# The mixers' order on three engines: scores, gelu, pool parts, transposes, out chunks and the taps of a convolution

## The chip, the cores and the metric

The kernel runs on one core of a Trainium2 chip. The metric is the device time of one execution in microseconds (us). TensorE is PE here, VectorE DVE, ScalarE ACT, GpSimd POOL, SyncE SP.

## What is computed

Two blocks of two layers each on a sequence of 256 tokens of width 1024. The first block has gated feed-forward parts around a forgetting attention and a dilated attention. The second block, twice, runs a mixer of four branches and a feed-forward part with a short convolution. The change touches the mixer alone:

```python
def second_block(x, ...):
    for l in range(DEPTH):                       # 2
        z = rms_norm_2(x, norm_mix_pre[l]) @ w_in[l]
        za, zq, zkv, zg, zc, zd = jnp.split(z, offsets, axis=-1)
        y_conv = conformer_conv(za, ...)         # a*sigmoid(gate), causal conv of 31 taps, layer norm, silu
        y_nsa = nsa_attention(q, ...)            # 4 heads: selected, windowed and compressed keys
        y_sgu = spatial_gating(zc, ...)          # gelu, layer norm of one half, 128x128 products in time
        y_pool = multiscale_pool(zd, ...)        # running means of 2, 4, 8, 16 and a product
        y = jnp.concatenate([y_conv, y_nsa, y_sgu, y_pool], axis=-1) @ w_out[l]
        x = x + rms_norm_2(y, norm_mix_post[l])
        ...
```

## The kernel before

All weights come as one stream of quarters of 128x1024, loaded by SP into a ring. Each quarter q is split in two for products of the precision wanted: ACT rounds it (split, L1055, w_hi), DVE subtracts (split, L1461, ring_lo), and PE makes three products of each pair, low by high, high by low, high by high (quarter, L444 to L446). ACT may split quarter q once PE is done with q-4; a split of DVE follows ACT's. There is no scheduler: each engine's program is a hand-written order, with waits on semaphores, and an engine does its instructions in that order. So what stands behind a wait waits too.

In mixer(l) quarters 0 to 15 of it (part(j, r), four 512-wide column groups j) make z; quarters 16 to 23 are the output product, cut in chunks of 128 rows in the order pool (chunks 0 and 1), gating (2 and 3), attention (4 and 5), convolution (6 and 7). out_chunk(kk) is quarter 16+kk; the last three are done in down_last (L499 to L501). The pieces of which this text speaks:

- Attention: compressed() (L891, L892) makes the compressed keys; DVE copies them (L2040, L2041, kv_ready). scores(0) and scores(1) (L920, L925) are the scores of two heads each. For each head h DVE takes masked maxes(h) (L1962), ACT exps(h) (L1307), DVE weigh(h) (L1969, L1971), ACT weighed(h) (L1317, six parts), PE turn_probs(h) (L937, L940), DVE take_probs(h) (L1978, L1979), PE values(h) (L949 to L951). PE's turn_probs(0) writes where part(3, r) was summed, so it waits for the gelu's read of it.
- Pool: pooled() (L863), ACT's copy pT (L1346), mixed() (L871), ACT's pool_hi (L1357), DVE's pool_out (L2066). out_chunk(0) waits for pool_out.
- Gating: the gelu of part 3 (L1353, b_gelu), DVE statistics (L2058, L2061), ACT's root (L1361), DVE's norm (L2073 to L2081), gating() (L898), DVE's product ysg (L2091), turn_gating (L906), ACT's sgu_hi (L1369), DVE's sgu_out (L2098). out_chunk(2) waits for sgu_out.
- Convolution: DVE's taps(first, end), two instructions a tap (L1989, 128x256 each), 31 taps, spread over the order; the last signals conv_ready. Then PE's mean products (L1004), DVE's difference, ACT's square, PE's variance products (L1009), ACT's root (L1376), DVE's reciprocal (L2106), ACT's silu (L1381) and the two halves (conv_out), for which down_last waits at its chunk 6.

ACT changes its function table (ACT_TABLE_LOAD) where exponential, gelu, root and silu alternate; Copy needs no change. The functions print below with their line numbers; ACT's part of the mixer and DVE's part have the same name, mixer(l).

## Time and profile before

| | us |
|---|---|
| median of 3 runs | 1981.53 |
| lowest, highest | 1979.51, 1983.31 |
| profiled execution | 1979.86 |
| its span, first to last instruction | 1978.2 |
| first mixer, from its part(2, 3) to the start of chunk 6 | 1365.2 to 1443.4 |
| second mixer, the same | 1689.2 to 1767.6 |

Times in the rows count from the start of the span. In a timeline row stand start, duration, engine, line, operation, output and inputs, the number of instructions merged, and in brackets the idle time of the engine ahead of it with what ended it. Durations of neighbours overlap where an engine pipelines; the chain's rows count each moment once. The chain of what ended last follows the releases backward from the last instruction.

### The profile page before, as it was taken

What the parts mean: (1) busy time and instruction counts of PE and PEld (TensorE: products, weight loads), DVE (VectorE), ACT (ScalarE), POOL (GpSimd) and SP (SyncE); (2) the same over time, 40 slices, a digit from 0 to 9 for tenths busy, and PEclk for the clock granted to TensorE, in tenths of its full rate; (3) what the DMA queues carried; (4) which work ended last, traced back from release to release, by engine and by line L of the source; (5) the groups of instructions that cost most, each with busy time, mean ns of one, the idle gap of its engine ahead of it and who ended that gap; (6) DMA issues with size and microseconds to landing.
All of it is one profiled execution on the core that took longest, in us unless ns stands there. A gap on an engine that the chain in (4) does not pass through costs nothing.

```text
span 1978.2 us, 32149 instructions
## 1 busy us (share of the span) xinstructions
PE 1854.0 (94%) x11902; PEld 1654.1 (84%) x11902; DVE 1429.3 (72%) x2221; ACT 939.7 (48%) x1357; POOL 130.1 (7%) x168
## 2 busy tenths in 40 slices
PE   2999999899999999999999999999789998789998
PEld 2999877799989997888878799978579987659997
DVE  6778898677787778677665555556768865867984
ACT  2444465454435443455454444444564445654443
POOL 1001111000110000000000000000011200001110
PEclk8999999989998999899999999999899998999999
DMA  9777765357787777354540255554145554224453
GB/s 365 268 272 280 279 232 204 118 188 279 271 302 256 275 269 272 120 186 173 188 149 1 86 209 190 179 207 150 51 173 188 176 191 148 107 82 153 177 185 126
DMA packets 61539, 382.11 MB, mean 193 GB/s; under 512 B 6896, under 2 KB 6896, under 8 KB 24448
## 3 DMA queue, kind: packets, MB, share of 16 engines
q1 hardware_dynamic: 41040, 300.96, 42.2%
q0 software_dynamic: 19984, 77.93, 11.1%
q10 hardware_dynamic: 432, 2.08, 0.3%
q8 instruction: 56, 0.92, 0.2%
q14 instruction: 27, 0.22, 0.0%
HBM read 379.89 MB, written 1.05 MB: 193 GB/s over the span
## 4 chain that ended last, share of the span: by engine, by line
PE 86%; DVE 8%; ACT 3%; issue 2%; DMA 1%; SPq 0%; DVEq 0%; ACTq 0%
PE ps L478 13%; PE ps L479 13%; PE ps L480 13%; PE ps L444 11%; PE ps L446 11%; PE ps L445 11%; PE ps L762 1%; DVE arena L1989 1%; PE ps L499 1%; PE ps L525 1%; PE ps L501 1%; PE ps L500 1%; DMA arena<-in_mod 1%; DVE ring_lo L1461 1%; PE ps L550 1%
## 5 line engine op out<-in xcount | busy, mean ns | idle before, releaser
L1461 DVE TENSOR_TENSOR ring_lo<-ring,w_hi 128x1024 fp32r<-128x1024 f32 x534 | 648.7, 1223 | 354.2 <-ACT w_hi L1055 350.2
L1055 ACT ACTIVATE w_hi<-ring 128x1024 fp32r<-128x1024 f32 x556 | 586.7, 1059 | 633.9 <-PE ps L480 325.4
L478 PE MATMUL ps<-h_lo,w_hi 128*128 128x256 f32 x2112 | 601.5, 285 | 10.4 <-issue 5.9
L479 PE MATMUL ps<-h_hi,w_hi 128*128 128x256 f32 x2112 | 600.7, 284 | 0.0
L480 PE MATMUL ps<-h_hi,ring_lo 128*128 128x256 f32 x2112 | 600.5, 284 | 0.0
L478 PEld LDWEIGHTS ps<-h_lo,w_hi 128*128 128x128 f32 x2112 | 407.5, 193 | 12.0 <-issue 7.2
L479 PEld LDWEIGHTS ps<-h_hi,w_hi 128*128 128x128 f32 x2112 | 407.5, 193 | 0.0
L480 PEld LDWEIGHTS ps<-h_hi,ring_lo 128*128 128x128 f32 x2112 | 407.4, 193 | 0.0
L444 PE MATMUL ps<-w_hi,h_lo 128*128 128x512 f32 x604 | 247.9, 410 | 21.4 <-DVE h_lo L2066 6.8
L446 PE MATMUL ps<-w_hi,h_hi 128*128 128x512 f32 x604 | 240.6, 398 | 0.0
L445 PE MATMUL ps<-ring_lo,h_hi 128*128 128x512 f32 x604 | 240.4, 398 | 0.0
L444 PE MATMUL ps<-w_hi,hid_lo 128*128 128x512 f32 x456 | 180.0, 395 | 0.0
L446 PE MATMUL ps<-w_hi,hid_hi 128*128 128x512 f32 x456 | 177.5, 389 | 0.0
L445 PE MATMUL ps<-ring_lo,hid_hi 128*128 128x512 f32 x456 | 177.5, 389 | 0.0
L444 PEld LDWEIGHTS ps<-w_hi,h_lo 128*128 128x128 f32 x604 | 116.7, 193 | 50.0 <-DVE h_lo L2066 7.8
L1529 DVE SCALAR_TENSOR_TENSOR wc<-arena,cact,wc 128x512 f32<-128x512 f32 x192 | 143.8, 749 | 3.4
L446 PEld LDWEIGHTS ps<-w_hi,h_hi 128*128 128x128 f32 x604 | 116.4, 193 | 25.7
L445 PEld LDWEIGHTS ps<-ring_lo,h_hi 128*128 128x128 f32 x604 | 116.9, 194 | 22.8
L386 POOL DMA_DIRECT2D arena<-in_mod x128 | 68.1, 532 | 678.8 <-DVE wc L1529 513.1
L444 PEld LDWEIGHTS ps<-w_hi,hid_lo 128*128 128x128 f32 x456 | 85.6, 188 | 18.9 <-issue 1.4
L445 PEld LDWEIGHTS ps<-ring_lo,hid_hi 128*128 128x128 f32 x456 | 85.6, 188 | 18.9 <-issue 1.4
L446 PEld LDWEIGHTS ps<-w_hi,hid_hi 128*128 128x128 f32 x456 | 85.6, 188 | 17.9
(320 smaller groups left out, 1924.6 us busy)
## 6 DMA issues: line engine op xcount, KB each, us to landing
ring<-in_stream SPq DMA_DIRECT2D x278, 1024.0 KB, 4.8
arena<-in_mod POOLq DMA_DIRECT2D x128, 512.0 KB, 5.4
arena<-in_mod SPq DMA_DIRECT2D x3, 2048.0 KB, 17.2
gate<-in_wide POOLq DMA_DIRECT2D x3, 1536.0 KB, 10.1
arena<-in_nsaw POOLq DMA_DIRECT2D x2, 1072.0 KB, 8.9
arena<-in_mod SPq DMA_DIRECT2D x1, 1536.0 KB, 26.4
arena<-in_konst POOLq DMA_DIRECT2D x1, 1295.5 KB, 8.5
arena<-in_mixw POOLq DMA_DIRECT2D x2, 576.0 KB, 9.8
```

The source lines that it names most:

```text
L386: pool.dma_start(mring[:, r, :], a["mod"][q, :, r * QUARTER:(r + 1) * QUARTER]).then_inc(mod_in[r], 16)
L444: nc.tensor.matmul(dst, x_lo, hi, start=first(i), stop=False)
L445: nc.tensor.matmul(dst, x_hi, lo, start=False, stop=False)
L446: mm = nc.tensor.matmul(dst, x_hi, hi, start=False, stop=last(i))
L478: nc.tensor.matmul(dst, hi, x_lo, start=(r == 0 and i == 0 and b % 2 == 0), stop=False)
L479: nc.tensor.matmul(dst, hi, x_hi, start=False, stop=False)
L480: mm = nc.tensor.matmul(dst, lo, x_hi, start=False, stop=(r == 3 and i == 1 and b % 2 == 1))
L499: nc.tensor.matmul(dst, x_lo, hi, start=False, stop=False)
L500: nc.tensor.matmul(dst, x_hi, lo, start=False, stop=False)
L1055: nc.scalar.activation(w_hi[:, q % SPLITS, :], ring[:, half % SLOTS, (q % 2) * QUARTER:(q % 2 + 1) * QUARTER], ACT.Copy).then_inc(w_hi_rea ...
L1461: v.tensor_tensor(ring_lo[:, slot, cs], ring[:, slot, cs], w_hi[:, q % SPLITS, :], ALU.subtract).then_inc(w_lo_ready, 1)
L1529: ins = v.scalar_tensor_tensor(out=dst, in0=src, scalar=c, in1=tmp, op0=ALU.mult, op1=ALU.add)
```

## The change

It moves pieces of the three orders in mixer(l). On PE scores(1) goes ahead of mixed(), turn_probs(2) ahead of gating(), turn_gating() ahead of turn_probs(3), and the mean products of the convolution, with their wait for conv_ready, and values(3) ahead of out_chunk(2). On ACT split(16) goes ahead of the copy pT; a small gelu on one column loads the table ahead of the wait for part 3; split(17) and weighed(1) go behind gelu and pool_hi, split(18) behind the root, and later splits by one place, the last two together. On DVE taps 7 to 12 go ahead of split(14) and others are regrouped, maxes(2) and maxes(3) go ahead of weigh(1), pool_out and take_probs(0) ahead of the gelu's statistics, and weigh(3), split(19) and the splits of quarters 20 and 21 later. No product, tap or copy is added or removed; the small gelu is the only new instruction, once a mixer. The whole diff:

```diff
--- before.py
+++ after.py
@@ -978,8 +978,8 @@
                 scores(0)
                 pooled()
                 part(3, 2, bA)
+                scores(1)
                 mixed()
-                scores(1)
                 part(3, 3, bA)
                 pe.wait_ge(b_gelu, l + 1)
                 turn_probs(0)
@@ -990,19 +990,19 @@
                 turn_probs(1)
                 out_chunk(1)
                 values(1)
+                turn_probs(2)
                 gating()
-                turn_probs(2)
                 values(2)
+                turn_gating()
                 turn_probs(3)
-                turn_gating()
                 pe.wait_ge(sgu_out, l + 1)
-                out_chunk(2)
-                values(3)
                 pe.wait_ge(conv_ready, l + 1)
                 mean = k2[:, KONST2["mean"]:KONST2["mean"] + P]
                 for c in range(2):
                     mm = nc.tensor.matmul(ps[:, 6, 0:T], mean, cacc[:, c, :], start=(c == 0), stop=(c == 1))
                 mm.then_inc(mu_sum, 1)
+                values(3)
+                out_chunk(2)
                 out_chunk(3)
                 pe.wait_ge(csq_ready, l + 1)
                 for c in range(2):
@@ -1342,13 +1342,12 @@
                 nc.scalar.activation(hid[HD:P, 0:NCMP], ps[HD:P, 7, 0:NCMP], ACT.Gelu_apprx_tanh).then_inc(hid_ready, 1)
                 split(q0 + 15, q0 + 16)
                 exps(0)
+                split(q0 + 16, q0 + 17)
                 act.wait_ge(pool_sum, l + 1)
                 nc.scalar.activation(pT, ps[:, 7, :], ACT.Copy).then_inc(pool_copied, 1)
-                split(q0 + 16, q0 + 17)
                 exps(1)
                 weighed(0)
-                weighed(1)
-                split(q0 + 17, q0 + 18)
+                nc.scalar.activation(warm[:, :], eps_col, ACT.Gelu_apprx_tanh)
                 act.wait_ge(quarter_done, q0 + 16)
                 nc.scalar.activation(zg[:, :, :], ps[:, bA:bA + 2, :], ACT.Gelu_apprx_tanh).then_inc(b_gelu, 1)
                 act.wait_ge(pool_mix, l + 1)
@@ -1356,18 +1355,19 @@
                     o = COLS["pool_s"] + 2 * l + c
                     ins = nc.scalar.activation(h_hi[:, 6 + c, :], ps[:, 7, c * T:(c + 1) * T], ACT.Copy, scale=cols[:, o:o + 1])
                 ins.then_inc(pool_hi, 1)
-                split(q0 + 18, q0 + 19)
+                split(q0 + 17, q0 + 18)
+                weighed(1)
                 act.wait_ge(zvar_ready, l + 1)
                 nc.scalar.activation(lnv[:, 4:6], lnv[:, 0:4].rearrange("p (t w) -> p t w", t=NT)[:, :, 1], ACT.Sqrt, bias=ln_eps_col).then_inc(zstd_ready, 1)
+                split(q0 + 18, q0 + 19)
                 exps(2)
                 weighed(2)
-                split(q0 + 19, q0 + 20)
                 exps(3)
                 weighed(3)
-                split(q0 + 20, q0 + 21)
+                split(q0 + 19, q0 + 20)
                 act.wait_ge(sgu_T, l + 1)
                 nc.scalar.activation(h_hi[:, 4:6, :].rearrange("p c t -> p (c t)"), ps[:, 6, :], ACT.Copy).then_inc(sgu_hi, 1)
-                split(q0 + 21, q0 + 22)
+                split(q0 + 20, q0 + 22)
                 act.wait_ge(cd_ready, l + 1)
                 nc.scalar.activation(csq[:, :, :], cd[:, :, :], ACT.Square).then_inc(csq_ready, 1)
                 act.wait_ge(no_sum, NH * (l + 1))
@@ -2027,32 +2027,32 @@
                 split(q0 + 12, q0 + 13)
                 taps(3, 5)
                 split(q0 + 13, q0 + 14)
-                taps(5, 7)
+                taps(5, 13)
                 split(q0 + 14, q0 + 15)
-                taps(7, 10)
                 dve.wait_ge(d_copied, l + 1)
                 for k, (tt, b) in enumerate(branch):
                     src = gt[:, tt, :].rearrange("p (h b) -> p h b", b=3)[:, :, b]
                     late = k2[:, KONST2["late"]:KONST2["late"] + 1] if k == 4 else 1.0
                     tick.mark(v.tensor_scalar(g6[:, :, k], src, late, None, ALU.mult))
-                taps(10, 14)
                 dve.wait_ge(kv_sum, 3 * l + 3)
                 v.tensor_copy(kcT, ps[:, 6, 32:32 + NCMP])
                 v.tensor_copy(vc, ps[0:NCMP, 7, 64:64 + HD]).then_inc(kv_ready, 1)
                 split(q0 + 15, q0 + 16)
-                taps(14, 16)
                 maxes(0)
                 maxes(1)
-                taps(16, 17)
+                taps(13, 14)
                 weigh(0)
                 split(q0 + 16, q0 + 17)
+                maxes(2)
+                maxes(3)
                 weigh(1)
-                taps(17, 19)
-                maxes(2)
-                split(q0 + 17, q0 + 18)
-                maxes(3)
-                taps(19, 21)
-
+                taps(14, 16)
+                dve.wait_ge(pool_hi, l + 1)
+                for c in range(2):
+                    ins = v.scalar_tensor_tensor(out=h_lo[:, 6 + c, :], in0=ps[:, 7, c * T:(c + 1) * T], scalar=col("pool_s", 2 * l + c),
+                                                 in1=h_hi[:, 6 + c, :], op0=ALU.mult, op1=ALU.subtract)
+                ins.then_inc(pool_out, 1)
+                take_probs(0)
                 dve.wait_ge(b_gelu, l + 1)
                 for tt in range(NT):
                     tick.mark(v.bn_stats(bnst[:, tt * 6:tt * 6 + 6], zg[:, tt, C2:512]))
@@ -2060,15 +2060,8 @@
                 for tt in range(NT):
                     ins = v.bn_aggr(lnv[:, 2 * tt:2 * tt + 2], bnst[:, tt * 6:tt * 6 + 6])
                 ins.then_inc(zvar_ready, 1)
-                taps(21, 23)
-                dve.wait_ge(pool_hi, l + 1)
-                for c in range(2):
-                    ins = v.scalar_tensor_tensor(out=h_lo[:, 6 + c, :], in0=ps[:, 7, c * T:(c + 1) * T], scalar=col("pool_s", 2 * l + c),
-                                                 in1=h_hi[:, 6 + c, :], op0=ALU.mult, op1=ALU.subtract)
-                ins.then_inc(pool_out, 1)
-                take_probs(0)
-                split(q0 + 18, q0 + 19)
-                taps(23, 25)
+                split(q0 + 17, q0 + 18)
+                taps(16, 20)
                 dve.wait_ge(zstd_ready, l + 1)
                 tick.mark(v.reciprocal(lnv[:, 4:6], lnv[:, 4:6]))
                 tick.settle()
@@ -2079,25 +2072,27 @@
                 tick.mark(v.tensor_tensor(vn, vn, ln[0], ALU.mult))
                 tick.settle()
                 v.tensor_tensor(vn, vn, ln[1], ALU.add).then_inc(vn_ready, 1)
+                split(q0 + 18, q0 + 19)
                 weigh(2)
                 take_probs(1)
-                split(q0 + 19, q0 + 20)
-                weigh(3)
-                taps(25, 28)
+                taps(20, 22)
                 dve.wait_ge(sgu_sum, l + 1)
                 fv = ps[:, 6, :].rearrange("p (t n) -> p t n", t=NT)
                 for g in range(4):
                     gs = slice(g * HD, (g + 1) * HD)
                     ins = v.scalar_tensor_tensor(out=ysg[:, :, gs], in0=fv[:, :, gs], scalar=col("sgu_b", 4 * l + g), in1=zg[:, :, gs], op0=ALU.add, op1=ALU.mult)
                 ins.then_inc(sgu_ready, 1)
+                weigh(3)
                 take_probs(2)
-                split(q0 + 20, q0 + 21)
-                taps(28, TAPS)
+                taps(22, 24)
+                split(q0 + 19, q0 + 20)
                 flat = lambda w, c: w[:, c:c + 2, :].rearrange("p c t -> p (c t)")
                 dve.wait_ge(sgu_hi, l + 1)
                 v.tensor_tensor(flat(h_lo, 4), ps[:, 6, :], flat(h_hi, 4), ALU.subtract).then_inc(sgu_out, 1)
+                taps(24, 26)
                 take_probs(3)
-                split(q0 + 21, q0 + 22)
+                taps(26, TAPS)
+                split(q0 + 20, q0 + 22)
                 dve.wait_ge(mu_sum, l + 1)
                 v.tensor_tensor(cd, cacc, ps[:, 6, 0:T].unsqueeze(1).broadcast_to([P, 2, T]), ALU.subtract).then_inc(cd_ready, 1)
                 dve.wait_ge(no_hi, l + 1)
```

## Rows read from the trace of the kernel before

**Rows 1.** Both mixers' stretches: us, busy us of each engine, clock, DMA share, GB/s.

```profile
1365.20:1443.43 78.23, 63.50 (x438) 48.05 (x436) 55.15 (x157) 44.00 (x106) 0.00 (x0) 0.89 0.20 72
...
1689.20:1767.59 78.39, 62.35 (x442) 46.93 (x441) 56.19 (x160) 44.01 (x106) 0.00 (x0) 0.91 0.21 77
```

**Rows 2.** PE's timeline, first mixer: start, us, line, xcount, idle before and releaser.

```profile
1383.01 1.58 PE L920 MATMUL ps<-arena 64*128 64x256 f32 x16 [1.66 <-DVE arena L2041]
...
1400.24 0.96 PE L937 MATMUL ps<-konst,arena 128*128 128x128 f32 x6 [4.23 <-ACT wa L1353]
...
1405.34 0.79 PE L444 MATMUL ps<-w_hi,h_lo 128*128 128x512 f32 x1 [3.71 <-DVE h_lo L2066]
...
1423.15 0.65 PE L949 MATMUL ps<-arena 128*64 128x256 f32 x2 [1.52 <-DVE arena L1979]
```

**Rows 3.** PE in the chain (start us, us), both mixers; one timeline row.

```profile
1416.80 0.58 PE ps L949 x2
...
1418.82 1.94 PE ps L898 x16
...
1433.16 1.06 PE ps L1004 x4
...
1436.97 0.88 PE ps L1009 x4
...
1745.74 1.11 PE L949 MATMUL ps<-arena 128*64 128x256 f32 x2 [1.72 <-DVE arena L1979]
...
1749.39 0.81 PE ps L937 x6
```

**Rows 4.** VectorE: timeline and chain of both mixers, groups of the first.

```profile
1375.44 1.23 DVE L1461 TENSOR_TENSOR ring_lo<-ring,w_hi 128x1024 fp32r<-128x1024 f32 x1 [6.87 <-ACT w_hi L1055]
...
1376.66 2.38 DVE arena L1989 x6
...
L1962 DVE CUSTOM_DVE_ANT_0 arena<-ps,arena 128x256 f32<-128x256 f32 (+2 forms) x24 | 5.4, 285 | 0.0
...
1402.00 0.68 DVE arena L2058 x2
...
1402.69 0.25 DVE L2061 BATCH_NORM_AGGREGATE arena<-arena 128x2 f32<-128x6 f32 x2
...
1404.50 0.80 DVE h_lo L2066 x2
...
1420.79 1.13 DVE L2091 SCALAR_TENSOR_TENSOR wc<-ps,cols,wa 128x128 f32<-128x128 f32 x4 [0.94 <-PE ps L898]
...
1421.91 0.86 DVE arena L1978
...
1424.16 2.45 DVE L1989 SCALAR_TENSOR_TENSOR arena<-arena,cols 128x256 f32<-128x256 f32 x6
...
1732.80 0.09 DVE arena L2073
...
1735.10 0.11 DVE rsum L1969
```

**Rows 5.** ScalarE: chain and timeline of the first mixer.

```profile
1389.48 0.60 ACT arena L1346
...
1391.02 0.05 ACT arena L1307
...
1393.25 3.66 ACT L1317 ACTIVATE arena<-arena,rsum 128x256 f32<-128x256 f32 x12
...
1397.87 1.28 ACT L1353 ACT_TABLE_LOAD   x1
...
1400.09 0.83 ACT L1357 ACTIVATE h_hi<-ps,cols 128x256 fp32r<-128x256 f32 x2
```

**Rows 6.** Granted clock (PEclk, third from the end), two stretches, columns as in rows 1.

```profile
1405.34:1411.00 5.66, 5.66 (x13) 4.04 (x14) 5.55 (x12) 1.89 (x11) 0.00 (x0) 0.50 0.00 0
...
1746.00:1749.00 3.00, 3.00 (x10) 1.66 (x9) 3.00 (x7) 0.00 (x0) 0.00 (x0) 0.50 0.00 0
```

## The prediction

> **What bounds the kernel now.** First the busy times of each engine in the two stretches of the mixers [rows 1]. Where TensorE (PE) runs without a break nothing on VectorE (DVE) or ScalarE (ACT) shows; what this change can move must lie where PE waits, and here it does: 63.50 us of PE work in 78.23, and 62.35 in 78.39. Their DVE is busy for 55 to 56 us of 78, so PE and DVE take turns in setting the end. Next the order of PE's work in the first mixer with the idle time ahead of each piece [rows 2]: 1.66 us ahead of scores(0), which waits for DVE's kv_ready; 4.23 ahead of turn_probs(0), which waits for the gelu on ACT; 3.71 ahead of out_chunk(0), which waits for pool_out on DVE. The second mixer has the same shape, and I work out the first and count it twice.
>
> **Front part: the pieces that go early.** Each instruction of a tap takes 0.40 us (six in 2.38) [rows 4]. Taps 7 to 12 are twelve such, 4.8 us. They move ahead of split(14), where DVE sits idle for 6.87 us until ACT's w_hi [rows 4]. So they cost nothing there; if that idle were under 4.8 the rest would come back on kv_ready. kv_ready then follows the products of compressed() and no longer 14 tap instructions, and scores(0) starts when part(3,1) is done: 1383.01 less the whole 1.66, at 1381.35. Its 1.9 us put the first score at DVE at 1383.3. maxes costs 1.35 a head (5.4 us in 24 pieces for four heads) [rows 4]. exps(0) on ACT starts at 1384.6 and takes 2.4, a little over exps(1), split(16) and the copy pT 1.5 together (from 1389.48 to 1391.02) and exps(1) 2.3 (to 1393.25) [rows 5], weighed(0) 1.8 (twelve pieces, two heads, 3.66) [rows 5]: 1392.7. Then table load and gelu, 2.2 together (from 1397.87 to 1400.09) [rows 5], and 0.2 for the small activation of one column that calls the table (an estimate, under the 0.4 of one of 256 columns in pool_hi, two in 0.83): b_gelu at 1395.1 against 1400.1. PE took 13.0 us from scores(0) to the end of part(3,3) (1383.01 to 4.23 ahead of 1400.24) [rows 2], with a wait of mixed for pT in it that scores(1) now covers; it is done by 1394.3 at the latest, ahead of the gelu. turn_probs(0) follows at once and is over at 1396.4. pool_hi takes 0.7, pool_out on DVE 0.8 [rows 4, 5], with DVE ready by 1394.2, since maxes(2), maxes(3), weigh(1) and two taps fit in. out_chunk(0) starts at 1396.7, against 1405.34 [rows 2]. **So the front gains 8.6 us.** Its order costs nothing else: split(17) on ACT goes behind gelu and pool_hi, but out_chunk(1) needs it only at 1402.6.
>
> **Middle part: DVE sets the pace.** Between pool_out at 1396.7 and the last tap DVE has in its queue: four take_probs at 1.2 (0.86 for the larger of two copies, and PE goes on 1.24 after its start, at 1423.15), statistics 0.9 (0.68 and 0.25), the norm of the gating branch 2.3 (1732.80 to 1735.10), two weigh at 0.37 (an estimate from 0.11 for the first of its two small pieces), ysg 1.1, sgu_out 0.7, three splits at 1.13 (1.23 in the row, whose end lies over the next one's start), and taps 16 to 30, 30 instructions at 0.40 or 11.9 [rows 2, 4]. That is 26.0 us. Two waits lie in it. The first is for sgu_sum: take_probs(1) stands behind 3.2 us of taps, the gating norm, split(18) and weigh(2), so it ends at 1408.2, though PE has been done with out_chunk(1) since 1405.4; from there values(1) takes 2.0, turn_probs(2) 1.0 (0.81 for six of its eight) and gating 1.9 [rows 3], to 1413.3, while DVE has only two taps to do and idles for 3.5. The second, 0.4, is for sgu_hi: behind take_probs(2) PE owes values(2) and turn_gating, and ACT the copy. In sum the last tap ends at 1396.7 + 26.0 + 3.9 = 1426.6. In the kernel before the last six tap instructions begin at 1424.16 and end at the same 1426.6 [rows 4]. **The 8.6 us won in front do not reach conv_ready.**
>
> **End part: what waits for that.** Before, conv_ready is 6.5 us old when PE asks for it at 1433.16: out_chunk(2) and values(3) fill the time [rows 3]. After the change the mean products come ahead of both. PE is done with turn_probs(3) at 1419.6 and then has nothing allowed: a wait of 7.1 us, with values(3), out_chunk(2) and out_chunk(3) queued behind it. Then mean products 1.06, values(3) 2.03, two chunks at 2.75 (1434.22 to 1436.97 holds one) [rows 3]: the variance products start at 1426.6 + 0.05 + 1.06 + 2.03 + 5.5 = 1435.3, against 1436.97. All that follows hangs on them as before: csq is ready by 1430.5, ACT's and DVE's splits of the last quarters are in their old places behind it. So 1.7 us are won in a mixer, 3.4 in both, if the clock stays high.
>
> **The clock.** I expect that it does not stay there. The granted clock was 0.50, which is 1.2 GHz, for the 5.66 us from out_chunk(0) on in the first mixer, after the idle times of 4.23 and 3.71, and for 3.00 us from 1746.00 in the second, after one of 1.72 [rows 2, 3, 6]. A slow stretch gives away half of itself: 2.8 and 1.5, mean 2.2. The 7.1 us wait is longer than any of these, and I charge 2.2 a mixer, 4.4 in both, on work with nothing beside it (0 to 2.8 each as bounds). The middle has two waits of 2.8 us a mixer (for take_probs(1) and take_probs(2)), between transposes, values and gating. The row that it is nearest to is the 1.7 us wait among the same kinds in the second mixer: values then took 3.65 (1745.74 to 1749.39) instead of 2.02, 1.6 more [rows 3]. Here that lands on DVE, which waits for gating, and so on conv_ready. Of the two old waits ahead of values, 1.52 in the first mixer and 1.72 in the second, only the second lowered the clock [rows 2, 3]; the new ones are longer by over 1 us: I take three of four, 4.8 (none 0, all 6.4). The slow stretch at out_chunk(0) that goes away returns nothing, as DVE sets the middle.
>
> The Trainium skill (TensorE: Matmul & The Clock Gate, HAM oscillation) says that idle times between bursts of matmuls put the clock to its lower level each time, and asks for work kept contiguous; it speaks against a wait placed ahead of two ready chunks. The trace agrees with it in part: the clock fell behind the wait of 1.72 and not behind that of 1.52. [...]
>
> **The sum.** -3.4 + 4.4 + 4.8 = +5.8 us. The profiled execution took 1979.86 (span 1978.2), which is 1.67 under the median of 1981.53; I add to the median: 1987.3. Its own range, from no middle slow stretch and 1.5 at each end (-0.4) to all of them at 2.8 (+8.6), is 1981 to 1990.
>
> **Rivals.**
> (1) The middle keeps its clock: the waits of 2.8 leave it high, as the old wait of 1.52 did. -3.4 + 4.4 = +1.0, 1982.5, within 0.2%. For: that row. Against: the new waits are longer. Chance 0.2.
> (2) Faster: DVE has the taps done earlier than I place them. The place is the wait for sgu_sum. Each microsecond by which values(1), turn_probs(2) and gating come sooner takes one from conv_ready, up to 3.5 a mixer; then the wait ahead of the mean products is short enough to keep the clock, and the mixers give 3.4 + 7 = 10.4 at most, 3.4 at least: 1971.1 to 1978.1. It decides in favour from the point at which conv_ready comes before 1424.5, since below that even a slow end (2.2) leaves over 0.8 a mixer and with a clean clock over 3. For: PE starts its out chunks 8.6 us sooner, a large sum to lose entirely. Against: 26.0 us of DVE work behind pool_out leave only the 3.9 of waits to be won. Chance 0.2.
> (3) The change does nothing at the end: conv_ready stays at 1426.6 and PE reaches the variance products when it did, small delays at each hand-over eating the 1.7, the slow stretches being short. 1981.5. For: the agreement of both last taps. Against: no delay is seen of that size. Chance 0.1.
> The forecast has 0.5.
>
> About 0.2%, 4.0 us, is what a measurement tells from no change. Slower 0.5 (the forecast), within 0.2% 0.3 (rivals 1 and 3), faster 0.2 (rival 2). The range goes from 1977.5, just under the near edge of rival 2, to 1990.5, the end of the forecast's; what is left out is most of rival 2 and less than 0.05 above.
>
> **What would show it.** Right: idle ahead of scores(0) (L920) gone; out_chunk(0) some 15 us behind the start of scores(0), where it was 22; a wait of 6 to 9 us of PE for the last tap, ahead of the mean products (L1004 of before); DVE idle 3 to 5 us ahead of ysg; granted clock 0.50 right behind the long wait. Wrong: no wait ahead of the mean products; a front gain much under 8; the clock at 1.00 from gating to the end of the mixer; or a mixer stretch shorter than 76 us.

## The result, and the profile after

| | us |
|---|---|
| before, median of 5 runs (lowest, highest) | 1981.53 (1976.23, 1983.31) |
| after, median of 5 runs (lowest, highest) | 1992.28 (1990.68, 1995.87) |
| ratio | 1.0063, 95% interval 1.0043 to 1.0082 |
| forecast | 1987.3, range 1977.5 to 1990.5 |
| profiled executions, before and after | 1979.86 and 1992.28 |
| their spans | 1978.2 and 1990.6 |

The kernel became slower, as forecast, but by 10.75 us where the forecast had 5.8, and the time lies above the range. The two profiled executions differ by 12.4 us.

Where it lies is read first from the windows of the two mixers, up to the same instruction of their ends. The first two rows are the stretches of [rows 1] after the change. The others are pieces of them that the text comes to.

Windows of the kernel after: stretch, us, busy us of each engine (instructions), PEclk, DMA share, GB/s.

```profile
1363.66:1447.14 83.48, 69.47 (x437) 51.84 (x436) 55.33 (x157) 44.18 (x107) 0.00 (x0) 0.80 0.19 68
1694.20:1778.28 84.08, 66.71 (x444) 49.39 (x442) 56.74 (x160) 44.19 (x107) 0.00 (x0) 0.86 0.20 73
...
1395.97:1399.50 3.53, 3.53 (x10) 2.73 (x9) 3.50 (x10) 3.50 (x8) 0.00 (x0) 0.52 0.08 35
...
1421.00:1427.40 6.40, 0.00 (x0) 0.01 (x1) 6.40 (x16) 0.72 (x1) 0.00 (x0) 0.50 0.00 0
1427.42:1436.40 8.98, 8.98 (x22) 5.61 (x23) 3.47 (x4) 2.51 (x3) 0.00 (x0) 0.50 0.00 0
1437.00:1445.00 8.00, 8.00 (x36) 6.59 (x36) 2.88 (x3) 3.10 (x4) 0.00 (x0) 1.00 0.33 131
1758.59:1767.90 9.31, 9.31 (x22) 5.86 (x23) 3.46 (x4) 2.51 (x3) 0.00 (x0) 0.50 0.00 0
```

Both mixers are longer, 83.48 against 78.23 and 84.08 against 78.39. DVE and ACT are busy for the same time as before (55.3 and 56.7, 44.2). PE is busy for 6.0 and 4.4 us more, with about as many products. Products that only take longer mean a lower clock, and the clock says so: 0.80 and 0.86, where [rows 1] had 0.89 and 0.91. The fourth row is the wait itself: PE does nothing for 6.40 us, DVE does its last taps, and the clock is down already. The fifth and the last are the work behind the wait, all of it at 0.50, that is 1.2 GHz, for 9.0 and 9.3 us; the sixth shows the clock back at 1.00 from 1437.00, 3.5 us ahead of the variance products.

PE's waits of the kernel after, first mixer: us in total, how many, the longest.

```profile
PE ps L1002 <- DVE arena L1989: 6.5, 1, 6.5
...
PE ps L949 <- DVE arena L1979: 3.6, 2, 2.7
PE ps L937 <- ACT wa L1352: 1.8, 1, 1.8
...
PE ps L444 <- DVE h_lo L2052: 0.6, 1, 0.6
```

The first row is the forecast wait for the last tap, ahead of the mean products. The waits of [rows 2] in front are gone (1.66) or shorter (4.23 and 3.71, now 1.8 and 0.6).

PE's timeline of the kernel after, both mixers (columns as in [rows 2]).

```profile
1379.74 1.58 PE L920 MATMUL ps<-arena 64*128 64x256 f32 x16
...
1393.78 0.87 PE L937 MATMUL ps<-konst,arena 128*128 128x128 f32 x6 [1.83 <-ACT wa L1352]
1395.42 0.50 PE L444 MATMUL ps<-w_hi,h_lo 128*128 128x512 f32 x1 [0.55 <-DVE h_lo L2052]
...
1406.74 0.65 PE L949 MATMUL ps<-arena 128*64 128x256 f32 x2 [0.92 <-DVE arena L1979]
...
1414.29 1.11 PE L949 MATMUL ps<-arena 128*64 128x256 f32 x2 [2.71 <-DVE arena L1979]
...
1427.42 2.05 PE L1002 MATMUL ps<-arena 128*128 128x256 f32 x4 [6.52 <-DVE arena L1989]
...
1440.52 1.03 PE L1009 MATMUL ps<-arena 128*128 128x256 f32 x4
...
1737.31 1.12 PE L949 MATMUL ps<-arena 128*64 128x256 f32 x2 [2.54 <-DVE arena L1979]
...
1758.59 2.04 PE L1002 MATMUL ps<-arena 128*128 128x256 f32 x4 [6.52 <-DVE arena L1989]
...
1771.66 1.02 PE L1009 MATMUL ps<-arena 128*128 128x256 f32 x4
```

out_chunk(0) starts 15.7 us behind scores(0) (1379.74 to 1395.42), where it was 22.3. The same two products of values take 0.65 at the full clock and 1.11 or 1.12 at the lower one. From the mean products to the variance products it is 13.10 and 13.07 us.

DVE's timeline of the kernel after: where the mixer's measure below begins, the wait ahead of ysg, the last taps, where the measure ends, and the wait ahead of ysg in the second mixer.

```profile
1373.90 1.23 DVE L1461 TENSOR_TENSOR ring_lo<-ring,w_hi 128x1024 fp32r<-128x1024 f32 x1 [2.12 <-ACT w_hi L1055]
...
1411.62 1.13 DVE L2083 SCALAR_TENSOR_TENSOR wc<-ps,cols,wa 128x128 f32<-128x128 f32 x4 [3.35 <-PE ps L898]
...
1423.25 4.03 DVE L1989 SCALAR_TENSOR_TENSOR arena<-arena,cols 128x256 f32<-128x256 f32 x10
...
1442.09 1.75 DVE L2101 RECIPROCAL wb<-wb 128x256 f32<-128x256 f32 x1 [7.47 <-ACT wb L1376]
...
1743.79 1.13 DVE L2083 SCALAR_TENSOR_TENSOR wc<-ps,cols,wa 128x128 f32<-128x128 f32 x4 [4.96 <-PE ps L898]
```

**One measure for all kernels.** Starts of whole executions shift by some microseconds (split(14) of the first mixer starts between 1372 and 1381 us in the profiles here), so I measure a mixer from the start of split(14) on DVE to the start of the reciprocal of the convolution's root on DVE. It has three parts: to the start of the mean products, from there to the start of the variance products, and 1.57 us more (2.0 to 2.3 in some of the kernels below). Each is a difference of two starts in a timeline.

| profiled execution | last tap ends | mean products start | mean to variance | mixer |
|---|---|---|---|---|
| before, mixer 1 / 2 | 51.2 / 50.2 | 57.7 / 58.2 | 3.7 / 3.7 | 62.9 / 63.5 |
| after, 1 / 2 | 53.4 / 54.0 | 53.5 / 54.2 | 13.1 / 13.1 | 68.2 / 68.8 |

The 12.4 us between the spans are: 1.5 less up to split(14) of the first mixer, 5.25 more in the first mixer, 5.3 in the second, and 1.7 more both between the mixers (260.67 to 262.35) and behind the second (215.66 to 217.37). The last two lie in the norm behind each mixer, which the change doesn't touch; they come back below.

### The profile page after: what moved, and what is told of

Read it like the earlier page. It is cut to its first block, busy times and chain, and to the rows that moved or that the text cites. A ratio compares the mean times of both kernels' runs of the same rounds, so it can differ in the third digit from the quotient of the medians.

```text
span 1990.6 us, 32149 instructions
## 1 busy us (share of the span) xinstructions
PE 1866.9 (94%) x11902; PEld 1662.4 (84%) x11902; DVE 1429.7 (72%) x2221; ACT 939.9 (47%) x1359; POOL 130.1 (7%) x168
## 4 chain that ended last, share of the span: by engine, by line
PE 86%; DVE 8%; ACT 3%; issue 2%; DMA 1%; SPq 0%; DVEq 0%; ACTq 0%
PE ps L478 13%; PE ps L479 13%; PE ps L480 13%; PE ps L444 11%; PE ps L445 11%; PE ps L446 11%; PE ps L525 1%; PE ps L762 1%; PE ps L499 1%; PE ps L501 1%; PE ps L500 1%; DMA arena<-in_mod 1%; PE ps L550 1%; PE ps L788 1%; PE ps L775 1%
```

## The experiments

The theory: DVE's order sets the last tap at or behind its old time, so that the mean products, placed first, hold three ready pieces of PE behind them, and the waits lower the clock. The rivals: the clock has nothing to do with it and the wait alone costs; the early mean products are bad in any order; DVE's regrouped taps are the harm; the early gelu is. Times are medians, each with its ratio to the kernel before run beside it.

### Undo the end on PE alone

From the kernel after:

```diff
                 pe.wait_ge(sgu_out, l + 1)
+                out_chunk(2)
+                values(3)
                 pe.wait_ge(conv_ready, l + 1)
...
                 mm.then_inc(mu_sum, 1)
-                values(3)
-                out_chunk(2)
                 out_chunk(3)
```

> The changed kernel with one thing undone: out_chunk(2) and values(3) stand ahead of the wait for conv_ready again. Theory (the loss is the 6.5 us wait for the last tap with two chunks queued behind it, and the 9.4 us at 1.2 GHz that follow): PE has no wait of over 2 us for conv_ready, the variance products come 6 to 9 us earlier in each mixer, 1974 to 1981 us. Rival (the loss is in the middle, where gating, transposes and values run slow and DVE waits for them; what PE does at the end only fills time): 1989 to 1993 us.

Measured: 1973.55, ratio 0.9972 (0.9958 to 0.9986). That is 18.7 under the kernel after and 6 under the kernel before beside it, half a microsecond below the expected range. So one exchange on PE makes the whole loss and hides a gain of the rest. PE's timeline and the window behind its wait:

```profile
1425.71 1.13 PE L1004 MATMUL ps<-arena 128*128 128x256 f32 x4 [0.50 <-DVE arena L1989]
```

```profile
1411.90:1420.90 9.00, 8.23 (x27) 5.72 (x28) 6.17 (x13) 4.94 (x10) 0.00 (x0) 0.50 0.00 0
...
1421.90:1430.00 8.10, 7.60 (x35) 5.50 (x34) 6.92 (x14) 1.42 (x3) 0.00 (x0) 1.00 0.00 0
```

The last tap comes as late as before the edit in mixer 1 (53.4) and later still in mixer 2 (57.5), but PE waits for it only 0.50 and 0.47. From mean to variance it is 3.7 in both. The mixers take 59.3 and 63.4. The clock still falls in the middle, and it is back at 1.00 by 1421.9, where PE has products to do and the kernel after has its wait.

At the end of the mixer the loss has two parts. With the mean products first, values(3) and out_chunk(2) stand between them and the variance products: 8.55 at the full clock (the fill of 30 products below) against 3.7 here, 4.8 a mixer. The slow clock adds to that 4.6 a mixer in the profiled execution of the kernel after, and 2.8 and 1.5 in another one (below).

### Fill the wait, change nothing else

In the kernel after, between the two waits; the products' results are read by nobody, and the wait for conv_ready stays:

```diff
                 pe.wait_ge(sgu_out, l + 1)
+                low_part(q0 + 18, None, 0)
+                for n in range(20):
+                    nc.tensor.matmul(ps[:, 6, :], h_hi[:, MIX_CHUNKS[2], 0:P], w_hi[:, (q0 + 18) % SPLITS, 0:512], start=True, stop=True)
                 pe.wait_ge(conv_ready, l + 1)
```

> The changed kernel with 20 products of 128x128 by 128x512 into a free PSUM bank, whose result nobody reads, in the long wait for conv_ready. It separates the clock from the wait: the wait ends when it did, and the work behind it finds a fast clock. Theory: slow stretch behind the wait gone or under 3 us, 4 to 5 us less in each mixer, 1982 to 1985 us. Rival (the slow clock behind the wait hides under the chain of csq and the variance, the wait itself is the whole loss): 1991 to 1994 us.

Measured: 1988.69, ratio 1.0044 (1.0027 to 1.0061), 3.6 under the kernel after: useless work made it faster. It lies between the two expected ranges and fits neither (1982 to 1985 for the theory, 1991 to 1994 for the rival). In its first mixer the fill ends 0.72 ahead of the last tap and mean to variance is 8.7 us instead of 13.1. In the second the last tap ends 55.9 after split(14), 1.87 of wait is left, the clock falls again, and it is 10.3.

The same with 30 products:

> The second experiment with 30 unread products in the long wait in place of 20. There the first mixer had 0.7 us of wait left and a fast clock behind it; the second had 1.9 us left, and the clock fell again. With 30 (about 2.3 us more) no wait is left in either. Theory (the slow clock behind the wait is worth 4 to 5 us a mixer): no slow stretch behind the products in either mixer, up to 1.6 us late by the products themselves, 3 to 9 us below the changed kernel run beside it. Rival (the clock falls there whatever PE does): within 2 us of the changed kernel, or above it.

Measured: 1987.83, ratio 1.0041 (1.0027 to 1.0055); its six times run from 1981.56 to 1991.71, and the profiled one is the fastest. PE's timeline, first mixer, and the window of the middle and the fill in the second mixer:

```profile
1418.79 0.65 PE L949 MATMUL ps<-arena 128*64 128x256 f32 x2 [2.71 <-DVE arena L1982]
...
1422.87 7.11 PE L1001 MATMUL ps<-w_hi,h_hi 128*128 128x512 f32 x30 [0.54 <-DVE h_lo L2094]
...
1429.82 1.03 PE L1005 MATMUL ps<-arena 128*128 128x256 f32 x4
...
1438.35 1.03 PE L1012 MATMUL ps<-arena 128*128 128x256 f32 x4
```

```profile
1729.00:1755.00 26.00, 21.77 (x120) 16.34 (x118) 21.89 (x50) 12.79 (x41) 0.00 (x0) 1.00 0.11 41
```

Here the clock is at 0.50 for 3 us at out_chunk(0) in both mixers (as in the third row of the first fence) and doesn't fall again up to the end of the mixer, though the wait of 2.71 is there. The last tap ends 51.2 us after split(14) in both mixers, mean to variance is 8.53 and 8.55, and both mixers take 61.54. This is the changed order at the full clock: 1.4 and 1.95 us shorter than before. The sum without its clock terms had 1.7. The whole profiled execution still took 1981.56, since it begins 2.9 later and has 2.1 more between the mixers than the one before. The medians say less: against the kernel after measured beside it (below) the fill gains 3.7 us. Each of the two gains, 3.6 and 3.7, is near the noise; that both fills agree makes the sign safe (eleven times each in all, medians 4.3 apart). A likely reason for so little is that 30 products take longer than the wait when the clock is down already; no profile shows such an execution.

### The kernel after once more

> The changed kernel as it is, beside the one with 30 unread products on the same chip, so that the two are compared without a change of chip: 1990 to 1995 us, 10 to 13 above the kernel before, if the first measurement holds; 1985 or less would make the sizes of all comparisons with it smaller.

Measured, with no edit: 1991.54, ratio 1.0061 (1.0046 to 1.0076), six times from 1987.19 to 1995.54; the profiled one is the fastest. PE's timeline and two windows, which begin with the mean products and end where the clock rises:

```profile
1426.21 2.05 PE L1002 MATMUL ps<-arena 128*128 128x256 f32 x4 [6.52 <-DVE arena L1989]
...
1437.54 1.03 PE L1009 MATMUL ps<-arena 128*128 128x256 f32 x4
...
1756.48 2.04 PE L1002 MATMUL ps<-arena 128*128 128x256 f32 x4 [6.52 <-DVE arena L1989]
...
1766.53 1.03 PE L1009 MATMUL ps<-arena 128*128 128x256 f32 x4
```

```profile
1426.21:1431.60 5.39, 5.38 (x14) 3.08 (x14) 2.78 (x3) 0.63 (x1) 0.00 (x0) 0.50 0.00 0
1756.48:1759.50 3.02, 3.02 (x7) 1.80 (x8) 2.77 (x3) 0.22 (x1) 0.00 (x0) 0.50 0.00 0
```

The waits are the same to the hundredth, and what they cost is not:

| profiled execution, mixer | last tap ends | slow behind the wait | mean to variance | mixer |
|---|---|---|---|---|
| after, 1 | 53.4 | 9.0 | 13.10 | 68.2 |
| after, 2 | 54.0 | 9.3 | 13.07 | 68.8 |
| after once more, 1 | 54.0 | 5.4 | 11.33 | 67.0 |
| after once more, 2 | 52.2 | 3.0 | 10.05 | 64.0 |
| 30 products in the wait, 1 / 2 | 51.2 / 51.2 | 0 / 0 | 8.53 / 8.55 | 61.5 / 61.5 |

Each microsecond of slow clock behind the wait costs a half, and each late tap goes into the mixer one to one. The two columns together give the last column: 68.2 less 61.5 is 2.2 of late taps and 4.6 behind the wait, less 0.1 from the tap to the products.

What makes the taps late can be read too. Windows of the kernel after, second mixer, from out_chunk(0) to the wait ahead of values(1), and behind that wait:

```profile
1725.97:1737.00 11.03, 8.79 (x42) 6.30 (x42) 10.86 (x25) 8.85 (x25) 0.00 (x0) 1.00 0.14 48
1737.50:1740.50 3.00, 3.00 (x9) 1.73 (x9) 1.33 (x4) 2.88 (x15) 0.00 (x0) 0.50 0.52 216
```

Behind the same waits of 1.8 and 0.55 out_chunk(0) ran at 0.52 in the first mixer and at 1.00 in the second. Where it is slow, PE reaches values(1) late, waits 0.9 to 1.1 there and keeps its clock, and DVE waits 3.35 ahead of ysg. Where it is fast, PE waits 2.54, the clock falls, and DVE waits longer (4.96 in the row above). The ten mixers of the five profiles with this order of the middle (after, once more, end undone, 20 and 30 products) are of these two kinds, six of the first and four of the second, and the four have the latest last taps: 54.0, 54.0, 55.9 and 57.5, against 51.2 to 53.4.

### The early mean products in the kernel before

```diff
                 pe.wait_ge(sgu_out, l + 1)
-                out_chunk(2)
-                values(3)
                 pe.wait_ge(conv_ready, l + 1)
...
                 mm.then_inc(mu_sum, 1)
+                values(3)
+                out_chunk(2)
                 out_chunk(3)
```

> The kernel before with only the end of PE's order as in the change: mean products and values(3) ahead of out_chunk(2). There sgu_out comes later than conv_ready (1428.1 against 1426.6), so PE has nothing to wait for in addition. Theory (the order costs only where conv_ready is the later of the two): within 3 us of the kernel before, 1979 to 1984 us. Rival (this order costs in itself, by the clock or by the chunk's distance from its weights): 1987 us or more.

Measured: 1978.64, ratio 0.9993 (0.9982 to 1.0004). The edit that costs 18.7 us in the new order costs nothing in the old one. PE's waits of that kernel have no row for the last tap, but this:

```profile
PE ps L1002 <- DVE h_lo L2098: 1.4, 1, 1.4
```

It is the wait for sgu_out, which was there before: in the old order conv_ready is older than sgu_out. So the place of the mean products isn't bad in itself; it is bad where the last tap is the later of the two.

### The early taps alone

In the kernel before, taps 7 to 12 ahead of split(14) and tap 13 behind kv_ready:

```diff
-                taps(5, 7)
+                taps(5, 13)
                 split(q0 + 14, q0 + 15)
-                taps(7, 10)
...
-                taps(10, 14)
...
-                taps(14, 16)
+                taps(13, 16)
```

> The kernel before with DVE's taps 7 to 12 moved into its idle time ahead of split(14), nothing else. Theory (the front gain is real but needs the whole front: kv_ready 4.4 us earlier gives scores(0) its 1.7 us and the scores reach DVE sooner, then the gelu comes 3 to 4 us earlier by ACT's old order): idle ahead of scores(0) gone, 1 to 4 us less a mixer, 1972 to 1978 us. Rival (DVE's total sets the end and waits elsewhere take up what is moved): within 2 us of the kernel before.

Measured: 1976.75, ratio 0.9979 (0.9967 to 0.9992). The idle time ahead of scores(0) is gone, the waits of 4.2 and 3.1 stay, and the mixers are 2.8 and 3.7 shorter (60.1 and 59.8). The taps in front are no harm; they are a gain of their own (3.8 us under the kernel before beside it).

### The gelu late

The version with the end undone, with ACT's gelu behind weighed(0), weighed(1) and split(17), as before the change:

```diff
                 weighed(0)
-                nc.scalar.activation(warm[:, :], eps_col, ACT.Gelu_apprx_tanh)
+                weighed(1)
+                split(q0 + 17, q0 + 18)
                 act.wait_ge(quarter_done, q0 + 16)
...
-                split(q0 + 17, q0 + 18)
-                weighed(1)
```

> The first of the experiments (the change with the chunk ahead of the mean products) with ACT's old order around the gelu: weighed(0), weighed(1), split(17), then table load and gelu, without the small activation. Theory (the gelu's time sets pool_out, and from pool_out DVE's queue runs to the last tap without slack, so each microsecond passes to the end): gelu and out_chunk(0) 4 to 5 us later, 7 to 10 us more in both mixers, 1980 to 1984 us. Rival (the waits of the middle absorb it): within 3 us of the first, 1971 to 1977 us.

Measured: 1982.95, ratio 1.0014 (1.0001 to 1.0027), 9.4 more than with the early gelu (8 by the ratios). PE waits 4.7 us ahead of turn_probs(0) where it waited 1.8. The early gelu is a gain too, once the end doesn't wait.

### DVE: what stands in front of take_probs(1) and take_probs(2)

Two edits on the version with the end undone, the second on top of the first:

```diff
                 split(q0 + 17, q0 + 18)
-                taps(16, 20)
                 dve.wait_ge(zstd_ready, l + 1)
...
                 take_probs(1)
-                taps(20, 22)
+                taps(16, 22)
                 dve.wait_ge(sgu_sum, l + 1)
```

> The first of these kernels (chunk ahead of the mean products) with taps 16 to 19 moved from ahead of the gating norm to behind take_probs(1) on DVE. Theory (PE's 2.8 us wait for take_probs(1) and DVE's 3.4 to 5.0 us wait for gating are two sides of one bad order, and the first lowers the clock): the PE wait ahead of values(1) falls under 1 us, DVE's wait ahead of ysg under 2, the last tap comes 2 to 4 us earlier, and the time is 2 to 6 us below the first of these kernels. Rival (with the chunk in front PE sets the end and taps no longer matter): within 1.5 us of it.

```diff
                 taps(16, 22)
+                weigh(3)
+                take_probs(2)
                 dve.wait_ge(sgu_sum, l + 1)
...
                 ins.then_inc(sgu_ready, 1)
-                weigh(3)
-                take_probs(2)
```

> The fourth kernel (chunk ahead of the mean products, taps 16 to 19 behind take_probs(1)) with weigh(3) and take_probs(2) on DVE ahead of the wait for gating's sum. Theory (PE's 2.7 us wait ahead of values(2) is DVE standing at gating's sum with the next copy queued behind it, and it is this wait that lowers the clock for the 10 us behind it): the wait falls under 1 us, the slow stretch there is gone or under 4 us, the last tap comes 2 to 4 us earlier, 3 to 8 us less than the fourth kernel. Rival (the clock falls by the kind of work, transposes and half-array products, not by the wait): the slow stretch stays and the gain is under 2 us.

Measured: 1970.14, ratio 0.9949 (0.993 to 0.9968), and 1965.82, ratio 0.9929 (0.9914 to 0.9944). The steps of 3.4 and 4.3 us overlap in their intervals; the 7.7 of both together don't. The mixers of the profiles go with them: 59.3 and 63.4, then 58.2 and 58.1, then 55.5 and 55.5. With the first, values(1) doesn't wait, and DVE waits 0.72 ahead of ysg instead of 3.35; the wait of 2.71 ahead of values(2) and a slow stretch of 10 us behind it are still there. With the second that wait is 0.78 (0.95 in the second mixer), and the middle keeps the full clock:

```profile
1418.83 0.65 PE L949 MATMUL ps<-arena 128*64 128x256 f32 x2 [0.78 <-DVE arena L1979]
...
1429.92 1.44 PE L1004 MATMUL ps<-arena 128*128 128x256 f32 x4 [1.72 <-DVE arena L1989]
```

```profile
1409.00:1429.00 20.00, 17.62 (x100) 12.52 (x99) 18.76 (x45) 11.49 (x39) 0.00 (x0) 1.00 0.16 53
```

The last tap ends 48.6 us after split(14), 5 us sooner than after the change. PE is sooner too, waits 1.72 for it, and the clock still falls there: mean to variance is 5.3, where 3.7 is the full clock. take_probs(2) had stood behind a wait for gating that it doesn't need.

Now both DVE edits with the mean products early again on PE, which is the kernel after with a better DVE:

> The changed kernel, its mean products still ahead of out_chunk(2), with both edits of DVE's order (taps 16 to 19 behind take_probs(1), weigh(3) and take_probs(2) ahead of gating's sum). It is the sixth experiment with the early mean products put back. Theory (the early mean products cost what PE waits for the last tap and the slow clock behind that wait, whatever DVE does before): DVE's last tap comes 5 to 6 us earlier than in the change, PE is ready earlier too, so a wait of 5 to 7 us stays, and the time is 1976 to 1986 us, 10 us or more above the sixth experiment. Rival (with the clock kept high in the middle the late wait no longer matters): 1966 to 1972 us.

Measured: 1981.1, ratio 1.0 (0.9989 to 1.0011): 15.3 more than the same kernel with the mean products behind out_chunk(2) and values(3) (14 by the ratios). The last tap is 5 us earlier than in the kernel after, and the wait is longer (7.6, where 5 to 7 were expected), since PE too is sooner there:

```profile
1420.62 2.04 PE L1002 MATMUL ps<-arena 128*128 128x256 f32 x4 [7.63 <-DVE arena L1989]
```

Last, the other direction, out_chunk(3) ahead of the mean products as well:

```diff
                 values(3)
+                out_chunk(3)
                 pe.wait_ge(conv_ready, l + 1)
...
                 mm.then_inc(mu_sum, 1)
-                out_chunk(3)
                 pe.wait_ge(csq_ready, l + 1)
```

> The sixth experiment with out_chunk(3), too, ahead of the wait for conv_ready. Theory (there PE still waits up to 1.7 us for the last tap, which out_chunk(3) can fill; but then csq is waited for, for 2 us, ahead of the variance products): between 2 us less and 1 us more than the sixth. Rival (any wait ahead of the mean products lowers the clock for the end, so that filling it gains more): 3 us or more below the sixth, under 1963 us.

Measured: 1965.12, ratio 0.9922 (0.9908 to 0.9936). It is the best version: 27 us under the kernel after and, by the ratio, 15 under the kernel before beside it. PE doesn't wait for the last tap. In the first mixer the clock is still down at out_chunk(0), for 3.4 us, and then holds to the end of the mixer; in the second it holds throughout. The first:

```profile
1400.00:1440.00 40.00, 35.19 (x175) 25.54 (x174) 33.25 (x63) 26.06 (x60) 0.00 (x0) 1.00 0.15 53
```

Its wait went to the variance products, 1.4 for ACT's square. Its mixers are 1.1 shorter than those of the version with both DVE edits and one chunk ahead of the mean products; the medians differ by 0.7, which these runs don't resolve.

## Why the prediction was right in its sign and wrong in its size

**The front, right.** 8.6 us were to be won up to out_chunk(0), with out_chunk(0) some 15 behind scores(0). It came to 15.7 against 22.3, 6.6, and the start of scores(0) gained the rest: it lies 5.84 behind split(14) now (1373.90 to 1379.74) and lay 7.57 behind it (1375.44 to 1383.01). That is 8.4 in all.

**DVE sets the middle, right.** The last tap was put at its old place, 51.2 us after split(14), if the clock stays. It is 51.2 in both mixers of the version with 30 products. (DVE's terms add to 25.8 and not to 26.0, which changes nothing here.) The 8.4 us of the front did not reach conv_ready. DVE's idle time ahead of ysg, forecast at 3 to 5, is 3.35 in the row above and 4.96 in the second mixer.

**The middle's clock, right in sum.** The forecast had 2.4 a mixer. The last tap came at 53.4 and 54.0, that is 2.2 and 2.8 late, and at 54.0 and 52.2 when the kernel ran once more: 2.2 late on average. The two waits of 2.8 were to be there in both mixers. The one ahead of values(2) was, at 2.7; the one ahead of values(1) was 2.5 only where out_chunk(0) kept its clock, in one mixer of each profile, and 0.9 and 1.1 in the other. So three of four slow stretches came about in each profile, as counted. But the fourth was missing because out_chunk(0) was slow in that mixer, and the forecast had that stretch gone. That the sum fits is luck in part, and its bound was too low: 3.2 a mixer at most, where the last tap of the same middle was 4.7 late with 20 products and 6.3 with the end undone. Rival 1, a middle that keeps its clock, did happen with 30 products, in the presence of the same waits of 2.71. It is a matter of the execution, not of the wait's length alone.

**The wait at the end, right.** 7.1 forecast (6 to 9), 6.5 measured in all four mixers, and the clock was low behind it.

**The price of that wait: the step that failed.** "The 7.1 us wait is longer than any of these, and I charge 2.2 a mixer, 4.4 in both" with 2.8 as the bound. At the full clock mean to variance is 8.55. It was 13.1 twice in the profiled execution, which is 4.6 a mixer and 9.1 in both, and 2.8 and 1.5 when the kernel ran again. The mean of the four is 3.3, and two of them lie outside the bounds. I took the size from slow stretches of 5.66 and 3.00 us behind the old waits [rows 6], and the stretches here were 3.0 to 9.3 us, though the same sentence said that this wait is longer than those. The kernel before had such a spread already, in rows that I didn't use:

```profile
1401.00:1411.00 10.00, 6.29 (x17) 4.19 (x15) 9.86 (x25) 6.17 (x16) 0.00 (x0) 0.50 0.00 0
...
1728.96:1731.50 2.54, 2.54 (x6) 2.06 (x7) 2.54 (x4) 1.89 (x11) 0.00 (x0) 0.50 0.00 0
```

The low clock of the first mixer was there for 10.0 us, the wait of 3.71 included, and not for the 5.66 of [rows 6] alone; and in the second mixer out_chunk(0) was slow for only 2.54, behind waits of much the same length (4.19 and 3.13). The upper bound should have come from the work that stands behind the wait: it takes 8.55 at the full clock, so at half the clock throughout it would take 8.55 more.

**What the sum left out.** The norm behind each mixer took 1.7 us more in both places. Windows of the slow stretch behind the first mixer in the kernel after:

```profile
1457.50:1467.50 10.00, 7.52 (x34) 7.12 (x35) 8.70 (x17) 7.56 (x17) 1.89 (x3) 0.50 0.91 322
```

and of the kernel before:

```profile
1455.80:1458.90 3.10, 3.10 (x15) 3.10 (x16) 2.14 (x3) 1.78 (x5) 1.17 (x2) 0.50 1.00 276
```

From mixer 1's reciprocal to mixer 2's split(14) it is 260.7 to 260.8 in four profiles (before, the end undone, the early mean in the old order, the gelu late), 262.3 to 263.1 in seven, and 265.0 in two (the early taps alone, the kernel after once more). Two slow stretches go with these three groups. One is that of the norm: 3 us long in the four; 10 in four of the seven and in the two. The other is a stretch of nearly 7 us just ahead of mixer 2's split(14), which the four don't have, and which the other three of the seven (with 7 in the norm) and the two do. The kernel after once more and the kernel before there:

```profile
1698.60:1704.50 5.90, 5.90 (x46) 5.28 (x45) 3.38 (x9) 2.36 (x4) 0.00 (x0) 0.50 0.22 87
```

```profile
1692.00:1699.00 7.00, 7.00 (x147) 6.50 (x147) 1.60 (x5) 1.95 (x4) 0.00 (x0) 1.00 0.40 153
```

Behind the second mixer it is 215.5 to 215.7 where the norm's slow stretch is 3 or 7 us long, and 217.4 to 217.9 where it is 10. So these microseconds go with the clock too, but at places that the change doesn't touch. Faster kernels than before are in each of the three groups, so the mixer's order alone doesn't set them; but both profiles of the kernel after have the 10 us in both places, and there is one profile of the kernel before. Whether the change makes them more frequent, and what picks the one or the other, is open.

**The balance.** The profiled executions differ by 12.4, and the forecast was 5.8. Of the 6.6 between, 4.7 are the price of the end's slow stretches (9.1 instead of 4.4), 3.4 the two norm stretches, 0.3 the middle, less 1.5 for the earlier start and 0.3 for a shorter way from the last tap to the mean products than with the fill (0.14 against 0.28, twice). In the other profiled execution of the same kernel the two mixers took 131.0 together, 4.6 more than before, which is near the forecast; 6.1 came outside them and 3.4 went ahead of them. The end's term alone would have given 1989.6 at its mean of four (3.3 a mixer), which is inside the range, and 1992 at the 4.6 of the profiled execution. So the mechanism was right, and the medians hold a price of the clock that I set too low at the end, and a slow clock in the norm that the sum had at nothing, with shares that two profiles can't assign. How much of the 10.75 is the clock is only bounded: filling the wait gives back 3.6 and 3.7 by the medians, and 6.7 and 7.3 a mixer (late taps included) between the best profile with a fill and the profile of the kernel after.

**Rival 2**, faster by an earlier last tap, named the right place: the wait for sgu_sum. With what stood in it unneeded moved away, the last tap came 5 us sooner. But its claim that the end then loses its cost fell: with the mean products early the wait grew to 7.6 and mean to variance took 10.5 and 10.9. It is out_chunk(2) and values(3) behind that wait that cost, whenever the tap comes.

**Rival 3** fell: the small delays it needed weren't there (61.54 without the clock's part, against 62.9 and 63.5 before).

The Trainium skill (TensorE: Matmul & The Clock Gate, HAM oscillation) asks for bursts of matmuls without idle time between, and the runs agree in the direction: the two best versions are those with the shortest waits in the middle and at the end. The waits that this section tells of are longer than those of the middle, so it doesn't decide about them. Here the clock fell in or just behind the wait of 2.71 ahead of values(2) in all four mixers of the kernel after, and in neither mixer of the version with 30 products.

## What to carry to other kernels

In a hand-written order, ask of each wait which ready work stands behind it on its engine, and put that work ahead; an instruction may be moved early only if its operand is then the older one, and this order of two operands is what another part of the same change can turn round. On TensorE bound the price of a wait by all the work behind it that sets the end, run at half the clock, not by the slow stretches seen behind shorter waits. Where a single slow stretch can be 3 or 9 us long, profile twice before a microsecond is assigned to anything.

## What the runs showed of the hardware that was not expected

- Behind the same wait of 6.52 us the clock stayed at 0.50 for 3.0, 5.4, 9.0 and 9.3 us of uninterrupted products.
- The clock fell before the long wait, not in it, in all four mixers of the kernel after. It is at 0.50 in one piece from the wait of 2.71, or up to 1.3 us behind it, over transposes, values, the long wait and the work behind it, 22.8 us in the first mixer and 20, 17 and 14 in the other three:

```profile
1413.60:1436.40 22.80, 15.59 (x44) 9.84 (x45) 14.46 (x28) 7.37 (x13) 0.00 (x0) 0.50 0.00 0
```

- Twenty or thirty products that nobody reads made the kernel 3.6 and 3.7 us faster.
- Waits as short as 1.83 and 0.55 with eight transposes between them were followed by 3.5 us at 0.52 in the first mixer (the third row of the first fence above), and by none in the second (1.00 for 11.03 us).
